# Sparse attention's score products with the queries' high and low parts stacked along the contraction

## Chip, core and metric

The kernel runs on one core of one Trainium2 chip. The metric is the device time of one execution in microseconds (us). TensorE (PE) multiplies, VectorE (DVE), ScalarE (ACT) and GpSimd (POOL) do the elementwise work, and SyncE (SP) issues nearly all DMAs. Every engine runs its own instructions in the order in which they are written and waits on semaphores for the others.

## What is computed

The reference is two transformer blocks in a row on 512 positions of 1024 channels, in float32. The part that the change touches is in the first block: an attention of 8 heads of 64 channels which share one head of keys and values, and in which each query sees only the 128 keys that an indexer has chosen for it.

```python
def dsa_attention(q, k, v, qi, ki, wi):        # q: 8 heads x 64, k and v: one head of 64
    ...
        score = jnp.einsum('bqh,bqhs->bqs', wib.astype(jnp.float32), rel)
        score = jnp.where(causal[None], score, -jnp.inf)
        _, sel = lax.top_k(score, topk)         # topk = 128
        ...
        logits = jnp.einsum('bqhd,bqkd->bqhk', qb, k_sel).astype(jnp.float32) * (HEAD_DIM ** -0.5)
        logits = jnp.where(valid[:, :, None, :], logits, -jnp.inf)
        p = jax.nn.softmax(logits, axis=-1).astype(v.dtype)
        return jnp.einsum('bqhk,bqkd->bqhd', p, v_sel)
```

Beside it stands a second branch of the same block: a gated input `u`, a causal convolution of 31 taps over 4 chunks of 128 channels, a layer norm and a silu. Both branches meet in the product with `w_out`.

## The kernel before

**Numbers in two parts.** A float32 operand is kept as a rounded high part and a low part (the remainder), both of TensorE's fast type. A product of two such operands is three matmuls into one bank: high by high, high by low, low by high. The helper `three` (lines 1556 to 1560) does that, so in the profile the three have the lines L1558, L1559 and L1560 wherever they are used.

**Weights.** `load` (L438) brings a unit of weights into one of two halves of `RAW`; ACT rounds it into `WH` (L550), POOL subtracts it into `WL` (L1113), and PE multiplies (L1436, L1437 with `WH`, then L1442 with `WL`). A load waits until POOL has done the unit two before it (`w_lo`).

**The sparse stage.** It has 32 tiles: 4 groups `c` of 8 tiles `t`. A group is a chunk of 128 query channels, which is two heads; `half = t // 4` chooses the head (64 partitions), `t % 4` the block of 128 queries, and a tile has (t % 4 + 1) * 128 keys. The keys stand twice, in partitions 0 to 63 and 64 to 127 of `KSH` (high) and `KSL` (low). For tile n, PE runs in this order: `scores` of tile n + 3 (three matmuls of 64 rows, and one of 128 rows, L1583, which adds the mask `SEL` through an identity); `convolve_beside`, nine full matmuls of the convolution of chunks 2 and 3 into `ST` (tiles 0 to 10 and 12 to 22); `turn`, the transposes of the softmax of tile n (L1595); and `values`, the products with V for the tiles before. ACT takes the exponentials (L685) and the high part of the turned tile (`PTH`, L697). DVE takes the maximum (`NMX`, L2216), the reciprocal and the scaling (L2221, L2223), the low part (`PTL`, L2228), and per tile for n below 23 one tap of the convolution of chunks 0 and 1 (`CV`, L2128, two instructions).

**POOL beside it.** `diagonals(j)` (L1146) makes eight diagonal matrices of taps, high and low, for PE's convolution; it waits until PE has used the set two before. `queries(c)` (L1189, L1191) splits query chunk c into `AQH[b]` and `AQL[b]`, b = c % 2: chunks 0 and 1 while the weights `memk` are worked on, chunks 2 and 3 between the diagonals. Buffer 0 goes by the names `QSH` and `QSL` in the profile. `scores` waits for `staged` at t = 0.

**SP.** Its list is loads only here: `memk` (8 units), `memv` (8), then `outa` (8 units of `w_out`).

**The later layer ("fox").** In the second block another attention already works with stacked parts: SP copies 64 rows of high and low parts between partitions (`stack`, L511, twelve copies of 128 KB a group; `biases`, L515), and `scores` there is two full-height matmuls (L1585, L1586) and one with an identity (L1587).

Of the kernel before, what the change touches and what calls it, by code (L numbers as in the profile page):

```python
# [16 lines left out]
F32 = mybir.dt.float32  # L17
# [104 lines left out]
def build_program(nc, A, out):  # L122
    ctx = ExitStack()
    with ctx:
        first = (nc.sbuf_base + 127) // 128 * 128

        def at(name, shape, dt, offset):
            return nc.alloc_sbuf_tensor_at(name, shape, dt, offset=first + offset)
# [4 lines left out]
        def sem(name):  # L133
            return ctx.enter_context(nc.semaphore(name))
# [23 lines left out]
        AQH = [QSH[0], at("AQH1", [P, T], F32R, 43008)]  # L158
        AQL = [QSL[0], at("AQL1", [P, T], F32R, 45056)]
# [216 lines left out]
        cvs_in, k_lo = sem("cvs_in"), sem("k_lo")  # L376
# [57 lines left out]
        def _(sp):  # L434
# [16 lines left out]
            for name, w in (("memk", w_k), ("memv", w_v), ("outa", w_out[:, 0:4, :]), ("outb", w_out[:, 4:8, :]),  # L451
# [13 lines left out]
                with sp.Fori(name == "oc", 4) as i:  # L465
                    for s in range(2):
                        load(unit_at(name, i, s), s, w[:, :, bass.ds(i * 2 * P + s * P, P)])
# [642 lines left out]
        def _(pool):  # L1110
# [75 lines left out]
            def queries(c, b, first, last):  # L1186

                free("sparse", c, first)
                pool.tensor_copy(AQH[b][:], DS[:, bass.ds(c + 4, 1), :])  # L1189
                pool.drain()  # L1190
                pool.tensor_tensor(AQL[b][:], DS[:, bass.ds(c + 4, 1), :], AQH[b][:], ALU.subtract).then_inc(staged, 1)  # L1191
# [9 lines left out]
            for j in range(8):  # L1201
                remainder(START["memk"] + j, j % 2)
                if j in (3, 5):
                    queries(j // 4, j // 4, True, False)
# [7 lines left out]
            queries(2, 0, False, False)  # L1212
            for j in range(5, 8):
                diagonals(j)
            queries(3, 1, False, False)
# [209 lines left out]
        def _(pe):  # L1425
# [136 lines left out]
            def scores(kind, c, b, t):  # L1562
# [4 lines left out]
                if kind == "fox":  # L1567
                    if t == 0:
                        pe.wait_ge(stacked[0], 96 * (c + 1))
                        pe.wait_ge(stacked[1], 96 * (c + 1))  # L1570
                        pe.wait_ge(bias_in, 96 if c else 32)
                    if t % TB == 0:
                        pe.wait_ge(staged, STAGED[kind] + 2 * c + half + 1)
                elif t == 0:
                    pe.wait_ge(staged, STAGED[kind] + c + 1)
# [4 lines left out]
                elif kind == "sparse":  # L1580
                    rows = slice(half * 64, half * 64 + 64)
                    three(s[:, 0:nk], AQH[b][rows, q], AQL[b][rows, q], KSH[0][rows, 0:nk], KSL[0][rows, 0:nk], True, False)
# [139 lines left out]
            pe.wait_ge(k_lo, 1)  # L1722
# [1158 lines left out]
```

## Time and profile before

| | us |
|---|---|
| median of 3 runs | 2156.45 (2152.4 to 2157.42) |
| the profiled execution | 2157.53 |
| its span in the trace | 2155.7 |
| PE busy | 1979.7 (92%) |
| DVE busy | 1110.4 (52%) |
| POOL busy | 1047.3 (49%) |
| the sparse stage in the trace, first scores to the last `PTL` | 202 to 319 |

The profile gives starts in us from the start of the span. A matmul's recorded duration includes the time in the array, so what a matmul costs a busy PE is the distance from its start to the start of the next one. PEclk is the clock granted to TensorE as a share of 2.4 GHz; 0.50 is its lower level of 1.2 GHz. "Idle before" is what an engine waited, with the instruction that ended the wait.

### The profile page before, as it was taken

What the parts mean: (1) busy time and instruction counts of PE and PEld (TensorE: products, weight loads), DVE (VectorE), ACT (ScalarE), POOL (GpSimd) and SP (SyncE); (2) the same over time, 40 slices, a digit from 0 to 9 for tenths busy, and PEclk for the clock granted to TensorE, in tenths of its full rate; (3) what the DMA queues carried; (4) which work ended last, traced back from release to release, by engine and by line L of the source; (5) the groups of instructions that cost most, each with busy time, mean ns of one, the idle gap of its engine ahead of it and who ended that gap; (6) DMA issues with size and microseconds to landing.
All of it is one profiled execution on the core that took longest, in us unless ns stands there. A gap on an engine that the chain in (4) does not pass through costs nothing.

```text
span 2155.7 us, 30205 instructions
## 1 busy us (share of the span) xinstructions
PE 1979.7 (92%) x9963; PEld 1603.1 (74%) x9963; DVE 1110.4 (52%) x1820; ACT 733.4 (34%) x1233; POOL 1047.3 (49%) x573
## 2 busy tenths in 40 slices
PE   7888998989999999756899999999997799999997
PEld 5677766768887888545778888887876678888886
DVE  6787873654678696689434223132137844132232
ACT  4323234353322322435442222233235643222223
POOL 5465425526765744680454444446444235444442
PEclk9999999999999999889999999999999999999999
DMA  4233002323332333100233333334345413333332
GB/s 142 71 91 100 1 1 64 98 50 88 97 98 85 94 95 90 56 2 0 69 98 98 89 105 90 98 97 99 97 111 124 112 59 97 98 98 92 103 88 88
DMA packets 343417, 179.52 MB, mean 83 GB/s; under 512 B 27951, under 2 KB 335527, under 8 KB 343335
## 3 DMA queue, kind: packets, MB, share of 16 engines
q1 hardware_dynamic: 342592, 177.81, 29.4%
q8 instruction: 43, 0.70, 0.1%
q10 hardware_dynamic: 742, 0.68, 0.1%
q14 instruction: 40, 0.32, 0.1%
HBM read 162.73 MB, written 2.10 MB: 76 GB/s over the span
## 4 chain that ended last, share of the span: by engine, by line
PE 54%; issue 12%; POOL 9%; DVE 9%; POOLq 6%; DVEq 4%; ACT 4%; DMA 2%; SPq 1%; ACTq 0%
PE ACC L1436 15%; PE ACC L1442 15%; PE ACC L1437 15%; POOL WL L1113 7%; POOLq L1123 2%; DVEq L2222 1%; POOLq L1295 1%; POOLq L1283 1%; DVE PTL L2228 1%; ACT WH L550 1%; DMA RAW<-in_w_v_cross_dram 1%; PE ST L1558 1%; PE ST L1560 1%; PE ST L1559 1%; PE O L1558 1%
## 5 line engine op out<-in xcount | busy, mean ns | idle before, releaser
L1113 POOL TENSOR_TENSOR WL<-RAW,WH 128x1024 fp32r<-128x1024 f32 (+1 forms) x308 | 733.4, 2383 | 792.3 <-ACT WH L550 717.7
L1436 PE MATMUL ACC<-PH,WH 128*128 128x512 f32 x1248 | 495.6, 397 | 11.7 <-DVE PL L1962 3.1
L1437 PE MATMUL ACC<-PL,WH 128*128 128x512 f32 x1248 | 489.5, 392 | 0.0
L550 ACT ACTIVATE WH<-RAW 128x1024 fp32r<-128x1024 f32 (+1 forms) x308 | 317.8, 1034 | 490.1 <-PE ACC L1442 414.4
L1436 PE MATMUL ACC<-QH,WH 128*128 128x512 f32 (+1 forms) x1136 | 431.5, 384 | 23.8 <-ACT WH L550 18.1
L1437 PE MATMUL ACC<-QL,WH 128*128 128x512 f32 (+1 forms) x1136 | 426.8, 380 | 0.0
L1442 PE MATMUL ACC<-PH,WL 128*128 128x512 f32 x1248 | 311.1, 391 | 0.0
L1436 PEld LDWEIGHTS ACC<-PH,WH 128*128 128x128 f32 x1248 | 236.5, 190 | 71.1 <-issue 4.7
L1442 PE MATMUL ACC<-QH,WL 128*128 128x512 f32 (+1 forms) x1136 | 272.3, 380 | 9.6 <-POOL WL L1113 9.4
L1437 PEld LDWEIGHTS ACC<-PL,WH 128*128 128x128 f32 x1248 | 236.6, 190 | 49.3 <-issue 1.0
L1442 PEld LDWEIGHTS ACC<-PH,WL 128*128 128x128 f32 x1248 | 234.0, 188 | 52.6 <-issue 3.3
L1436 PEld LDWEIGHTS ACC<-QH,WH 128*128 128x128 f32 x1136 | 215.4, 190 | 75.6 <-issue 20.4
L1442 PEld LDWEIGHTS ACC<-QH,WL 128*128 128x128 f32 x1136 | 205.4, 189 | 55.2 <-POOL WL L1113 15.7
L1437 PEld LDWEIGHTS ACC<-QL,WH 128*128 128x128 f32 x1136 | 215.5, 190 | 39.0 <-issue 0.2
L2755 DVE TENSOR_TENSOR X<-X,ACC 128x512 f32 x48 | 33.0, 688 | 216.3 <-PE ACC L1442 216.3
L2745 DVE TENSOR_TENSOR H<-ACC,RS 128x512 f32<-128x512 f32 x64 | 44.3, 692 | 147.5 <-PE ACC L1442 147.0
L1122 POOL TENSOR_TENSOR SSQ<-SSQ,SQ 128x512 f32<-128x512 f32 x52 | 75.5, 1453 | 70.6 <-ACT SQ L557 63.8
L757 ACT ACTIVATE QH<-H 128x512 f32 (+1 forms) x54 | 34.2, 633 | 153.4 <-DVE H L2747 128.2
L697 ACT ACTIVATE PTH<-ACC 128x128 fp32r<-128x128 f32 (+2 forms) x112 | 48.1, 429 | 83.3 <-PE O L1560 55.5
L2228 DVE TENSOR_TENSOR PTL<-ACC,PTH 128x128 fp32r<-128x128 f32 (+2 forms) x112 | 53.3, 476 | 31.1 <-ACT PTH L697 30.8
L2128 DVE SCALAR_TENSOR_TENSOR CV<-U,VEC,CV 128x512 f32<-128x512 f32 x60 | 65.5, 1132 | 0.5
L757 ACT ACTIVATE PH<-H 128x512 f32 (+1 forms) x32 | 20.3, 633 | 128.6 <-DVE H L2747 128.6
(416 smaller groups left out, 2436.0 us busy)
## 6 DMA issues: line engine op xcount, KB each, us to landing
RAW<-in_mlp_w_dram SPq DMA_DIRECT2D x128, 512.0 KB, 4.0
RAW<-in_w_gate_dram SPq DMA_DIRECT2D x22, 512.0 KB, 3.7
RAW<-in_w_up_dram SPq DMA_DIRECT2D x22, 512.0 KB, 3.7
RAW<-in_w_in_dram SPq DMA_DIRECT2D x16, 512.0 KB, 3.8
RAW<-in_w_down_dram SPq DMA_DIRECT2D x16, 512.0 KB, 4.0
RAW<-in_ssm_w_glu_dram SPq DMA_DIRECT2D x16, 512.0 KB, 3.8
RAW<-in_w_kvf_dram SPq DMA_DIRECT2D x16, 512.0 KB, 3.9
RAW<-in_w_k_cross_dram SPq DMA_DIRECT2D x8, 512.0 KB, 4.0
```

Of the source, the lines that this page charges most:

```text
L550: act.activation(WH[:, s, 0:kc], RAW[:, s, 0:kc], ACT.Copy).then_inc(w_hi, 1)
L697: act.activation(PTH[:, first:first + kb, qb * P:(qb + 1) * P], TT[t % 2][:, 0:kb * P].rearrange("p (k q) -> p k q", q=P), ACT.Copy).then_ ...
L757: act.activation(hi[:, bass.ds(k, 1), :], to, ACT.Copy).then_inc(hid_hi, 1)
L1113: pool.tensor_tensor(WL[:, s, 0:kc], RAW[:, s, 0:kc], WH[:, s, 0:kc], ALU.subtract).then_inc(w_lo, 1)
L1122: pool.tensor_tensor(SSQ[:], SSQ[:], SQ[:, s, :], ALU.add).then_inc(sq_used, 1)
L1123: pool.drain()
L1436: pe.matmul(ACC[s][:, 0:n], WH[:, s, k, :], xh[:, k, :], start=(k == 0), stop=False)
L1437: pe.matmul(ACC[s][:, 0:n], WH[:, s, k, :], xl[:, k, :], start=False, stop=False)
L1442: mm = pe.matmul(ACC[s][:, 0:n], WL[:, s, k, :], xh[:, k, :], start=False, stop=(k == kc - 1))
L2128: ins = dve.scalar_tensor_tensor(CV[c][:], x, column("conv_b_w", BCH * k + c), CV[c][:], ALU.mult, ALU.add)
L2228: dve.tensor_tensor(PTL[to], TT[t % 2][:, 0:kb * P].rearrange("p (k q) -> p k q", q=P), PTH[to], ALU.subtract).then_inc(pt_lo, 1)
L2745: dve.tensor_tensor(h[:], ACC[s][:], RS[:], ALU.mult).then_inc(unit_out, 1)
```

## The change

The queries' high and low parts are put under one another. For each chunk SP copies 64-row halves of `AQH` and `AQL` into `AQ[b][:, half, :]`, a tile of 128 partitions in which 64 hold the high part of one head and the other 64 its low part (four copies of 128 KB a chunk, semaphore `joined`). Against `KSH`, whose two halves are the same keys, one full-height matmul then gives high by high plus low by high. Against `KLZ[half]`, which holds the keys' low part in the rows of the high queries and zeros in the others, a second gives high by low. `keys_low` on POOL makes `KLZ` once. `queries` no longer waits for exponentials but for the copies to have read its buffer, and SP's list now has the copies of chunks 0 and 1 ahead of the `outa` loads, those of chunks 2 and 3 behind the first two of them, and the other six `outa` loads last.

```diff
+        AQ = [at(f"AQ{b}", [P, 2, T], F32R, x) for b, x in enumerate((176128, 43008))]
+        AQH = [at(f"AQH{b}", [P, T], F32R, 25088 + 4096 * b) for b in range(2)]
+        AQL = [at(f"AQL{b}", [P, T], F32R, 27136 + 4096 * b) for b in range(2)]
+        KLZ = [at("KLZ0", [P, T], F32R, 47104), KSL[0]]
...
+                if name == "outa":
+                    for c in range(4):
+                        if c == 2:
+                            for s in range(2):
+                                load(START[name] + s, s, w[:, :, s * P:(s + 1) * P])
+                        sp.wait_ge(staged, c + 1)
+                        if c >= 2:
+                            sp.wait_ge(e_done, TILES["sparse"] + 8 * (c - 1) + 4)
+                        for u in range(2):
+                            mine, other = own(u), own(1 - u)
+                            for to, src in ((mine, AQH), (other, AQL)):
+                                sp.dma_start(AQ[c % 2][to, u, :].bitcast(F32), src[c % 2][mine, :].bitcast(F32)).then_inc(joined[c % 2], 16)
-                with sp.Fori(name == "oc", 4) as i:
+                with sp.Fori(name in ("outa", "oc"), 4) as i:
...
-            def queries(c, b, first, last):
-
-                free("sparse", c, first)
-                pool.tensor_copy(AQH[b][:], DS[:, bass.ds(c + 4, 1), :])
+            def queries(c):
+
+                if c >= 2:
+                    pool.wait_ge(joined[c % 2], 64)
+                b = c % 2
+                pool.tensor_copy(AQH[b][:], DS[:, c + 4, :])
                 pool.drain()
...
+            def keys_low():
+
+                pool.tensor_copy(KLZ[0][0:64, :], KSL[0][0:64, :].bitcast(F32))
+                pool.drain()
+                pool.memset(KLZ[1][0:64, :].bitcast(F32), 0.0)
+                pool.drain()
+                pool.memset(KLZ[0][64:P, :].bitcast(F32), 0.0)
+                pool.drain().then_inc(k_lo, 1)
...
                 remainder(START["memk"] + j, j % 2)
                 if j in (3, 5):
-                    queries(j // 4, j // 4, True, False)
+                    queries(j // 4)
+                elif j == 1:
+                    keys_low()
...
+                elif t == 0 and kind == "sparse":
+                    pe.wait_ge(joined[c % 2], 64 * (c // 2 + 1))
...
                 elif kind == "sparse":
-                    rows = slice(half * 64, half * 64 + 64)
-                    three(s[:, 0:nk], AQH[b][rows, q], AQL[b][rows, q], KSH[0][rows, 0:nk], KSL[0][rows, 0:nk], True, False)
+                    pe.matmul(s[:, 0:nk], AQ[b][:, half, q], KSH[0][:, 0:nk], start=True, stop=False)
+                    pe.matmul(s[:, 0:nk], AQ[b][:, half, q], KLZ[half][:, 0:nk], start=False, stop=False)
                     mm = pe.matmul(s[:, 0:nk], IDR[:], SEL[:, qb, 0:nk], start=False, stop=True)
```

On PE the block of a tile's scores stands between a turn and the convolution. Here are the turn of tile 0, the scores of tile 4 (128 keys) and the first of the convolution behind them, before:

```order
L1595 MATMUL ACC<-CST,E 128x128
L1558 MATMUL FOUR<-KSH,QSH 128x128
L1559 MATMUL FOUR<-KSL,QSH 128x128
L1560 MATMUL FOUR<-KSH,QSL 128x128
L1583 MATMUL FOUR<-SEL,IDR 128x128
L1558 MATMUL ST<-UH,DGH_120 128x512
```

and in the changed kernel, whose line numbers are higher (`AQ_76` is `AQ[0]`; the second product takes `KSL`, which is `KLZ[1]`, since tile 4 is of the second head):

```order
L1624 MATMUL ACC<-CST,E 128x128
L1610 MATMUL FOUR<-KSH,AQ_76 128x128
L1611 MATMUL FOUR<-KSL,AQ_76 128x128
L1612 MATMUL FOUR<-SEL,IDR 128x128
L1585 MATMUL ST<-UH,DGH_125 128x512
```

One matmul of the four is gone, and the two products left have 128 rows like their neighbours.

On SP the rows behind the last `memv` load are, before, the loop of the `outa` loads:

```order
L438 DMA RAW<-in_w_v_cross_dram 128x8x128
L465 REGISTER_ALU
L465 COMPARE_AND_BRANCH
L465 UNCONDITIONAL_BRANCH
L465 ISA
L438 ISA
L438 DMA RAW<-in_w_out_dram 128x4x128
```

and in the changed kernel:

```order
L478 DMA AQ_76<-AQH_78 64x512
L478 DMA AQ_76<-AQL_80 64x512
L478 DMA AQ_76<-AQH_78 64x512
L478 DMA AQ_76<-AQL_80 64x512
L478 DMA AQ_77<-AQH_79 64x512
L478 DMA AQ_77<-AQL_81 64x512
L478 DMA AQ_77<-AQH_79 64x512
L478 DMA AQ_77<-AQL_81 64x512
L440 DMA RAW<-in_w_out_dram 128x4x128 x2
```

Eight copies now stand between the last `memv` load and the first `outa` load.

## Rows read from the trace of the kernel before

**Rows 1.** Windows of the sparse stage: stretch, its length, busy time by engine, PEclk, DMA.

```profile
202.00:210.00 8.00, 7.95 (x24) 5.59 (x25) 4.07 (x10) 3.10 (x8) 1.92 (x1) 0.66 0.18 53
210.00:247.00 37.00, 37.00 (x177) 27.96 (x175) 31.82 (x56) 10.21 (x31) 15.05 (x9) 0.98 0.00 1
247.00:252.00 5.00, 1.34 (x7) 0.79 (x6) 4.85 (x5) 0.91 (x2) 3.46 (x2) 1.00 0.00 0
252.00:260.00 8.00, 8.00 (x24) 5.55 (x24) 6.48 (x14) 2.42 (x7) 0.00 (x0) 0.57 0.00 0
260.00:302.00 42.00, 42.00 (x207) 31.94 (x207) 36.27 (x73) 13.89 (x41) 10.29 (x6) 1.00 0.00 1
```

**Rows 2.** Timeline of PE: scores of 256, 512 and 128 keys and what follows.

```profile
229.08 0.38 PE L1558 MATMUL FOUR<-KSH,AQH 64*128 64x256 f32 x1
...
229.85 0.40 PE L1558 MATMUL ST<-UH,DGH 128*128 128x512 f32 x1
...
236.64 0.50 PE L1558 MATMUL FOUR<-KSH,AQH 64*128 64x512 f32 x1
...
237.86 0.39 PE L1558 MATMUL ST<-UH,DGH 128*128 128x512 f32 x1
238.10 0.40 PE L1559 MATMUL ST<-UL,DGH 128*128 128x512 f32 x1
...
240.58 0.40 PE L1560 MATMUL O<-PTH,VSL 128*128 128x512 f32 x1
240.91 0.32 PE L1558 MATMUL FOUR<-KSH,AQH 64*128 64x128 f32 x1
...
241.55 0.45 PE L1558 MATMUL ST<-UH,DGH 128*128 128x512 f32 x1
```

**Rows 3.** Timeline of PE in the later layer: full-height scores of 256 keys.

```profile
1634.67 0.28 PE L1585 MATMUL FOUR<-R,L 128*128 128x256 f32 x1
1634.79 0.28 PE L1586 MATMUL FOUR<-R,L 128*128 128x256 f32 x1
```

**Rows 4.** Timelines of DVE, POOL and PE around the wait of tile 11.

```profile
246.31 4.70 DVE L2128 SCALAR_TENSOR_TENSOR CV<-U,VEC,CV 128x512 f32<-128x512 f32 x2
253.12 1.40 DVE L2128 SCALAR_TENSOR_TENSOR CV<-U,VEC,CV 128x512 f32<-128x512 f32 x2
```

```profile
248.10 2.36 POOL L1146 TENSOR_TENSOR DGL<-CST,WCL 128x1024 fp32r<-128x1024 f32 x1
```

```profile
251.87 0.66 PE L1595 MATMUL ACC<-CST,E3sparse 128*128 128x128 f32 x4 [3.66 <-DVE E3sparse L2223]
```

**Rows 5.** Timelines of ACT and PE where the sparse stage begins.

```profile
200.43 1.06 ACT L550 ACTIVATE WH<-RAW 128x1024 fp32r<-128x1024 f32 x1 [1.19 <-DMA RAW<-in_w_out_dram]
201.74 0.38 ACT L674 ACTIVATE VM<-ACC 128x256 f32 x1 [0.25 <-PE ACC L1442]
```

```profile
202.05 0.29 PE L1558 MATMUL FOUR<-KSH,QSH 64*128 64x128 f32 x1 [0.45 <-ACTq L759]
```

**Rows 6.** The later layer's copies: SP's timeline, and a window of them.

```profile
1628.21 0.61 SPq L511 DMA_DIRECT2D R<-KLS  x1
```

```profile
1626.00:1630.00 4.00, 3.86 (x16) 3.27 (x15) 3.55 (x11) 3.12 (x10) 0.00 (x0) 0.50 0.89 204
```

**Rows 7.** Timelines of POOL and ACT in `memk`, and POOL's memset by line.

```profile
151.99 0.61 POOL L1189 CAST QSH<-DS 128x512 fp32r<-128x512 f32 x1
...
153.99 2.38 POOL L1113 TENSOR_TENSOR WL<-RAW,WH 128x1024 fp32r<-128x1024 f32 x1
```

```profile
151.13 1.06 ACT L550 ACTIVATE WH<-RAW 128x1024 fp32r<-128x1024 f32 x1 [1.29 <-DMA RAW<-in_w_k_cross_dram]
```

```profile
L1409 POOL MEMSET VSH<- 128x1024 f32 x1 | 1.0, 952 | 0.2 <-issue 0.2
```

**Rows 8.** Timelines of POOL and PE: chunk 3's queries, and their first use.

```profile
281.74 1.55 POOL L1191 TENSOR_TENSOR AQL<-DS,AQH 128x512 fp32r<-128x512 f32 x1
```

```profile
290.59 0.33 PE L1558 MATMUL FOUR<-KSH,AQH 64*128 64x128 f32 x1
```

More of the change, by code:

```diff
@@ L157, in build_program @@
         VSL = [at("VSL", [P, TB, 2, P], F32R, 190464), at("VSL1", [P, TB, 2, P], F32R, 77824)]
-        AQH = [QSH[0], at("AQH1", [P, T], F32R, 43008)]
-        AQL = [QSL[0], at("AQL1", [P, T], F32R, 45056)]
+        AQ = [at(f"AQ{b}", [P, 2, T], F32R, x) for b, x in enumerate((176128, 43008))]
+        AQH = [at(f"AQH{b}", [P, T], F32R, 25088 + 4096 * b) for b in range(2)]
+        AQL = [at(f"AQL{b}", [P, T], F32R, 27136 + 4096 * b) for b in range(2)]
+        KLZ = [at("KLZ0", [P, T], F32R, 47104), KSL[0]]
         CST = at("CST", [P, NCST], F32, 194560)
@@ L375, in build_program @@
         pv_done = sem("pv_done")
-        cvs_in, k_lo = sem("cvs_in"), sem("k_lo")
+        cvs_in, k_lo, joined = sem("cvs_in"), sem("k_lo"), [sem("joined0"), sem("joined1")]
         staged = sem("staged")
@@ L1184, in free @@
                     pool.wait_ge(e_done, TILES[kind] + SIZE[kind] * (c - 1) + 4)
-            def queries(c, b, first, last):
-                free("sparse", c, first)
-                pool.tensor_copy(AQH[b][:], DS[:, bass.ds(c + 4, 1), :])
-                pool.drain()
-                pool.tensor_tensor(AQL[b][:], DS[:, bass.ds(c + 4, 1), :], AQH[b][:], ALU.subtract).then_inc(staged, 1)
+            def queries(c):
[3 more added lines that the diff above has]
+                pool.tensor_copy(AQH[b][:], DS[:, c + 4, :])
+                pool.drain()
+                pool.tensor_tensor(AQL[b][:], DS[:, c + 4, :], AQH[b][:], ALU.subtract).then_inc(staged, 1)
+            def keys_low():
[5 more added lines that the diff above has]
+                pool.drain().then_inc(k_lo, 1)
             def inputs_low(j):
@@ L1211, in _ @@
                 diagonals(j)
-            queries(2, 0, False, False)
+            queries(2)
             for j in range(5, 8):
                 diagonals(j)
-            queries(3, 1, False, False)
+            queries(3)
             for c in range(BCH):
@@ L1721, in _ @@
             pe.wait_ge(sel_ready, TB)
-            pe.wait_ge(k_lo, 1)
+            pe.wait_ge(k_lo, 2)
             pe.wait_ge(v_lo, 2)
```

## The prediction

> **What bounds the kernel now.** The change lives in one stage of the span, so I read the windows of that stage first and then the timelines of single engines in it. In [rows 1] PE is busy for 37.00 of 37 us from 210 to 247 and for 42.00 of 42 from 260 to 302: there PE alone sets the pace. From 247 to 252 it is busy for 1.34 us only. The reader should look at DVE beside it: 31.82 of 37, 4.85 of 5, 6.48 of 8 and 36.27 of 42 us. DVE is the second bound, close behind, and PE's hole at 247 is its doing: PE waits 3.66 us for the scaled exponentials of tile 11 [rows 4]. DVE is late there because two taps of the convolution took 4.70 us where the same two take 1.40 seven microseconds later; POOL made diagonals just then, and the taps' end comes right after the end of POOL's instruction (248.10 + 2.36 = 250.46) [rows 4]. Behind that hole the granted clock is 0.57 from 252 to 260, and it is 0.66 from 202 to 210 [rows 1].
>
> **What PE loses.** The cost of a block of scores is the distance from its first matmul to the first of the convolution [rows 2]: 241.55 - 240.91 = 0.64 us for 128 keys, 229.85 - 229.08 = 0.77 for 256, 237.86 - 236.64 = 1.22 for 512, and about 1.00 for 384, taken between its neighbours. The matmul ahead of the block is stretched too: 240.91 - 240.58 = 0.33 instead of 0.24 (238.10 - 237.86, same width). That 0.09 I give to every block. A full-height block is three matmuls like those of the later layer: 0.12 each for 256 keys (1634.79 - 1634.67) [rows 3] and, since that looks like a floor, 0.12 for 128; 0.24 for 512, and 0.18 for 384 between them. So the blocks become 0.36, 0.36, 0.54 and 0.72. The saving of four tiles is 0.28 + 0.41 + 0.46 + 0.50 + 4 x 0.09 = 2.0 us, and eight such fours make **16 us of PE's time** at the full clock.
>
> Most of this is not the matmul that goes. The third matmul itself is 0.12 + 0.12 + 0.18 + 0.24 = 0.66 us of each 2.0, 5.3 of the 16. The rest is what PE loses where it goes from 128 rows to 64 and back: about 0.1 us ahead of the block, 0.1 in its first matmul, and 0.1 to 0.2 at the mask matmul. These are my reading of the distances; no row before shows a full-height block inside the sparse stage.
>
> The Trainium skill, page "TensorEngine Tiling (Array Packing)", section Tiling Modes, says that going to another tiling mode drains TensorE. By that rule the border costs are real and vanish with the 64-row matmuls; without it the change would be worth only the 5.3 us of the third matmuls.
>
> **What of it reaches the end.** *The first four blocks* run back to back from 202.05 and nothing else is due: DVE is busy for 4.07 of 8 us [rows 1]. All of their 2.0 us counts, and since the clock falls among them I take **2.7** (bounds 2.0 to 4.0, all at full or all at half clock). *From 210 to 302* PE saves 24 blocks, 12 us. DVE has 12.6 us free in these 92 (5.2 + 0.15 + 1.5 + 5.7, [rows 1]), part of it the short gaps between its own instructions. So PE and DVE would be level, and level engines which hand each tile back and forth do not both run full. It is worse while POOL makes diagonals, which happens six times in the stage: a pair blocks DVE for some 2 to 3.3 us (4.70 - 1.40, [rows 4]), and PE uses up a set of eight taps in 2.67 tiles. In those tiles DVE is the bound as soon as PE is any faster. The room is in the tiles without diagonals. I take **2.5** (bounds 0 and 10: nothing, or DVE's free time less its own gaps), nearer to nothing because the only hole of PE that the trace has, [rows 4], is DVE's and stays. *After 302* four blocks are left, among waits of PE for DVE and ACT: **0.3**. Together 5.5 us.
>
> The Trainium skill, page "SBUF — State Buffer", on the SBUF ports, says that DVE and GpSimd share a pair of ports under an exclusive lock and the loser is blocked for the whole instruction. The trace agrees (4.70 us where 1.40 is usual [rows 4]). By that rule alone a faster PE buys nothing while POOL works; without it I would put the middle term near its upper bound.
>
> **What it adds.** *Copies ahead of the load.* SP issues a copy in 0.61 us, and while copies run, the queues move 204 GB/s at a share of 0.89 [rows 6]. Eight copies behind the last `memv` load take 8 x 0.64 = 5.1 us of SP, from about 193 to 198, where the first `outa` load went out at 197.6: 0.5 us late. Their 1.05 MB take 5.1 us of the queues, behind or among the 0.5 MB of that `memv` load, so the queues are free at about 200 to 201.5, and the `outa` unit may land 0.5 to 2.2 us later than at 200.43. Behind it in ACT's order stand the rounding (1.06 us) and the copy of `VM`, which has 0.25 us to spare, and PE's first scores wait for the semaphore that follows it [rows 5]. That puts the whole stage back by 0.3 to 2; I take **1.3**. The new wait on `joined` stands at the same place; chunk 0's four copies should have landed by about 199, so it is not last.
>
> *`keys_low`.* One copy of half the rows (0.61 for 128 rows of 512 [rows 7]; I count it whole), two memsets of 512 columns (half of 0.95 each [rows 7]) and three drains of some 0.15: 2.0 us on POOL behind unit 1 of `memk`. Unit 2's remainder comes 2.0 later, hence the load of unit 4 too. Unit 4 was rounded at 151.13 + 1.06 = 152.2, and POOL took it at 153.99 only [rows 7], since `queries(0)` stood ahead: 1.8 us of cover. What is left is 0.2; I take **0.3** (bounds 0 and 2.0, the cover gone).
>
> *Chunk 3.* Its low part is ready at 281.74 + 1.55 = 283.3 and PE wants it at 290.59 [rows 8]: 7.3 us. SP's wait, four issues and the landing take 0.1 + 4 x 0.64 + about 2 = 4.6, and PE gains up to 2 between. It is covered by 0.7 us or so; PE would stop in front of it with the convolution and the turn queued behind, and I price that at 0 (bounds 0 to 1). Chunk 2 has over 10 us. The six `outa` loads now go out at about 285 instead of 204; the first of them is needed after 320, and it costs nothing. `queries` of chunks 2 and 3 waits for copies long landed.
>
> Sum: -5.5 + 1.3 + 0.3 = **-3.9 us**. Against the profiled execution's 2157.5 that is 2153.6; its time is 1.1 above the median of the runs, so from the median it is 2152.5. I say 2153. A measurement of this kernel can tell about 0.3%, 6.5 us, from no change, so this counts as no change.
>
> **Rivals.** (A) *PE's gain goes through.* DVE was held up by PE, not only beside it, and the diagonals fall elsewhere: the middle term is 9, the clock does not fall at the start, which saves 1 more, and the time is 2156.5 - 2.7 - 1 - 9 - 0.3 + 1.6 = 2145. For it: DVE has 12.6 us free [rows 1]. Against: the lock. Chance 0.25. (B) *Only the third matmul counts.* The borders' 0.1 us are not due to the height; PE saves 5.3 in all, some 2 reach the end, less 1.6 of costs: 2156. The distances of [rows 2] speak against it. Chance 0.12. (C) *The clock falls more often: slower than before.* PE gets some 12 us of new waits for DVE. Behind the wait of 3.66 us [rows 4] eight microseconds ran at 0.57 [rows 1]; each such stretch costs PE about 3.4 us, of which DVE's slowness covers little. One more makes 2156, two 2159.5, three 2163; it is slower than before from the second on. Against: in the 79 us in which PE runs full the clock is 0.98 to 1.00, and the waits that I expect are spread and most of them shorter than that one. Chance 0.15 for one or two more, 0.06 for three. (D) *The `outa` load is 4 us late*, with the copies in front of all of it, 2155.5: chance 0.07. The forecast itself has 0.35.
>
> **How the numbers follow.** Faster by over 0.3% (below 2150) is A with the lower edge of the forecast, 0.28. Slower by over 0.3% (above 2163) is C with three stretches and what I have not seen, 0.08. The rest, 0.64, is within 0.3%. The range reaches from the near side of A to C with two stretches and some spread: 2146.5 to 2161.
>
> **What would show it.** In the profile after: blocks of scores of 0.36 and 0.72 us for 128 and 512 keys; the first scores at 203 to 204 instead of 202.05; DVE busy for nearly all of 212 to 300 with PE's waits named after the scaled exponentials or `PTL`; the turns of tile 3 some 1.5 us earlier than before and those of tile 25 some 4. The prediction is wrong if PE stays busy to the full (then B), if DVE's busy time shrinks (A), or if PEclk shows further stretches near 0.5 (C).

## The result, and the profile after

| | before | after |
|---|---|---|
| median, us | 2156.9 (5 runs, 2152.4 to 2157.5) | 2144.9 (5 runs, 2142.3 to 2145.3) |
| the profiled execution, its span | 2157.5, 2155.7 | 2142.3, 2140.5 |
| PE busy | 1979.7 | 1962.5 |
| DVE busy | 1110.4 | 1108.7 |
| POOL busy | 1047.3 | 1048.8 |

The ratio of the times is 0.9945 (95% interval 0.9931 to 0.9958): the change is 12.0 us faster, three times what was forecast (3.9) and below the range. Timed again beside the last experiments its ratio was 0.9958 (0.9943 to 0.9973). The first interval lies wholly below 0.997, so the change is faster by more than the 0.3% that can be told from none; the second alone, which reaches 0.9973, would leave that just open. The two share 0.9943 to 0.9958, 9 to 12 us.

Windows of the changed kernel, the stretches of [rows 1] (stretch, length, busy time and instructions of PE, PE's loads, DVE, ACT, POOL, then PEclk, DMA share, GB/s):

```profile
202.00:204.00 2.00, 1.32 (x10) 1.09 (x9) 0.00 (x0) 0.76 (x1) 0.23 (x1) 1.00 0.24 61
204.00:210.00 6.00, 6.00 (x32) 5.16 (x33) 4.12 (x11) 3.73 (x11) 2.40 (x1) 1.00 0.10 31
210.00:247.00 37.00, 30.89 (x158) 24.36 (x156) 35.54 (x56) 10.57 (x31) 18.49 (x10) 1.00 0.06 15
247.00:252.00 5.00, 2.92 (x8) 2.08 (x9) 4.70 (x11) 1.93 (x5) 0.00 (x0) 0.50 0.00 0
252.00:260.00 8.00, 8.00 (x38) 6.63 (x37) 6.84 (x16) 2.42 (x8) 0.00 (x0) 0.89 0.01 2
260.00:302.00 42.00, 38.37 (x200) 30.29 (x199) 37.49 (x76) 14.93 (x43) 10.38 (x6) 1.00 0.08 19
```

Three things differ from [rows 1]. The clock from 204 to 210 is 1.00, where 202 to 210 had 0.66. PE, which had been busy for 37.00 of 37 us, is busy for 30.89, and DVE has risen from 31.82 to 35.54. The hole near 247 and the lower clock behind it are still there, a little earlier.

The blocks of scores are as short as forecast. PE's timeline of the first four blocks (128, 256, 384, 512 keys), of the convolution behind them and of tile 0's turn:

```profile
203.95 0.30 PE L1610 MATMUL FOUR<-KSH,AQ 128*128 128x128 f32 x1 [0.45 <-ACTq L773]
...
204.31 0.33 PE L1610 MATMUL FOUR<-KSH,AQ 128*128 128x256 f32 x1
...
204.72 0.34 PE L1610 MATMUL FOUR<-KSH,AQ 128*128 128x384 f32 x1
...
205.25 0.40 PE L1610 MATMUL FOUR<-KSH,AQ 128*128 128x512 f32 x1
...
205.94 0.40 PE L1585 MATMUL ST<-UH,DGH 128*128 128x512 f32 x1
...
208.04 0.27 PE L1624 MATMUL ACC<-CST,E 128*128 128x128 f32 x1
```

0.36, 0.41, 0.53 and 0.69 us, 1.99 together; the forecast was 0.36, 0.36, 0.54 and 0.72, 1.98. What PE waited for from the turn of tile 0 to that of tile 22 (times in us, count, longest), where the kernel before had one wait (last line, from its own turns of tiles 0 and 22):

```profile
PE ACC L1624 <- DVE E2sparse L2252: 3.6, 3, 2.3
PE ACC L1624 <- DVE E3sparse L2252: 3.5, 2, 2.0
PE ACC L1624 <- DVE E L2252: 1.2, 1, 1.2
PE O L1585 <- DVE PTL L2257: 0.8, 3, 0.3
```

```profile
PE ACC L1595 <- DVE E3sparse L2223: 3.7, 1, 3.7
```

All of it is DVE's, before and after.

**A table of distances.** Times in a trace shift by some 2 us from execution to execution before the stage begins, so I compare distances between starts inside of it. *Start*: from the rounding of `memv`'s unit 6 to the first scores. *First*: from there to the turn of tile 0. Then turn of tile 0 to 11, 11 to 22, turn of tile 22 to the last tile's `PTL`, and from that to the next rounding of weights and on to the seventh after it. All in us, one trace each; the kernels of the experiments stand here too, and the last column is the ratio of their time to that of the kernel before, timed beside them.

| kernel | start | first | 0 to 11 | 11 to 22 | 22 to end | behind | on | ratio |
|---|---|---|---|---|---|---|---|---|
| before | 8.1 | 8.7 | 41.1 | 43.8 | 22.5 | 4.8 | 27.9 | |
| before_again | 9.1 | 8.8 | 41.0 | 43.8 | 22.6 | 4.7 | 27.8 | |
| after | 9.8 | 4.1 | 41.0 | 38.8 | 22.6 | 3.4 | 26.7 | 0.9945 |
| after_again | 9.8 | 4.1 | 40.9 | 38.8 | 22.6 | 3.4 | 26.7 | |
| after_five | 10.0 | 4.1 | 40.7 | 38.7 | 23.0 | 4.1 | 26.4 | 0.9958 |
| third_full | 9.7 | 4.7 | 39.2 | 39.3 | 22.4 | 3.4 | 26.5 | 0.9962 |
| first_four_64 | 9.8 | 7.6 | 39.3 | 38.8 | 22.6 | 3.4 | 26.7 | 0.9980 |
| rest_64 | 9.5 | 4.1 | 40.8 | 43.8 | 22.9 | 4.2 | 26.5 | 0.9991 |
| all_64 | 11.8 | 8.9 | 40.9 | 43.8 | 22.8 | 4.3 | 27.9 | 1.0006 |
| last_four_64 | 10.2 | 4.1 | 40.9 | 38.7 | 23.5 | 3.4 | 26.3 | |
| before_two_64 | 8.1 | 6.9 | 40.8 | 43.8 | 22.9 | 4.2 | 26.5 | 0.9997 |
| before_act_scales | 9.1 | 8.9 | 37.6 | 41.7 | 25.9 | 5.3 | 27.3 | 0.9984 |
| act_scales | 10.4 | 4.1 | 35.9 | 37.1 | 26.8 | 4.4 | 26.7 | 0.9958 |
| act_scales_23 | 10.6 | 4.1 | 35.8 | 37.8 | 22.9 | 4.9 | 26.7 | 0.9929 |
| chunk1_late | 9.8 | 4.1 | 40.5 | 38.6 | 22.6 | 3.4 | 27.8 | 0.9960 |
| copies_behind | 9.2 | 4.1 | 39.3 | 38.8 | 22.6 | 3.4 | 26.7 | 0.9953 |
| both | 9.2 | 4.1 | 35.8 | 36.9 | 23.4 | 4.3 | 26.4 | 0.9930 |
| no_diagonals | 10.4 | 4.1 | 32.0 | 36.0 | 22.4 | 3.4 | 27.9 | 0.9920 |

From before to after (first two rows against the next two) the sum is: start +1.2, first -4.7, 0 to 11 nothing, 11 to 22 -5.0, 22 to end nothing, behind -1.3, on -1.1. That is -10.9 of the 9 to 12.

### The profile page after: what moved, and what is told of

It reads as the page before. It is cut to its first block, busy times and chain, and to the rows that moved or that the text cites. A ratio compares the mean times of both kernels' runs of the same rounds, so it can differ in the third digit from the quotient of the medians.

```text
span 2140.5 us, 30157 instructions
## 1 busy us (share of the span) xinstructions
PE 1962.5 (92%) x9931; PEld 1595.0 (75%) x9931; DVE 1108.7 (52%) x1820; ACT 732.9 (34%) x1233; POOL 1048.8 (49%) x576
## 4 chain that ended last, share of the span: by engine, by line
PE 51%; issue 13%; DVE 10%; POOL 9%; POOLq 6%; DVEq 4%; ACT 4%; DMA 2%; SPq 1%; ACTq 0%
PE ACC L1463 16%; PE ACC L1469 15%; PE ACC L1464 15%; POOL WL L1127 7%; POOLq L1137 2%; DVE CV L2157 2%; DVE PTL L2257 1%; DVEq L2251 1%; POOLq L1310 1%; POOLq L1322 1%; ACT WH L564 1%; DVEq L2161 1%; DVE NMX L2245 1%; PE ST L1903 1%; POOL GC L1321 1%
## 5 line engine op out<-in xcount | busy, mean ns | idle before, releaser
L1463 PE MATMUL ACC<-PH,WH 128*128 128x512 f32 x1248 | 494.9, 397 | 10.2 <-DVE PL L1991 2.4
```

Of the source, the lines that this page charges most:

```text
L1463: pe.matmul(ACC[s][:, 0:n], WH[:, s, k, :], xh[:, k, :], start=(k == 0), stop=False)
```

## Experiments

### Second traces

The two kernels unchanged, and the changed one timed again.

> The kernel before once more, for a second trace. Theory 1 (the stretches at the lower clock belong to the kernel): the granted clock falls again at 204, 252, 316, 344, 382 and 416 us, 30.6 us of stretches that cost 15.3 us of PE time between 200 and 430. Theory 2 (they fall by chance from execution to execution): the first one at 204 or the three behind 340 are elsewhere or missing, and the landmarks of the sparse stage move by 2 to 5 us against the first trace.

> The changed kernel once more, for a second trace. Theory 1: the clock is at its full level from 202 to 245, falls once behind PE's holes at 246 and once at 336, and nowhere else up to 420. Theory 2: a stretch at the lower clock stands among the first four blocks of scores in this trace, the turn of tile 0 comes at 210 to 211 instead of 208.0, and the time is still 2142 to 2146, so that the clock is not where the gain is.

> The changed kernel unchanged, timed again beside the others: 10 to 12 us below the kernel before by the sum of the distances (1.2 later at the start, 4.7 and 5.1 to 6 less in the stage, 2.4 less behind it), first scores 9.8 us behind the rounding of unit 6, 4.1 us to the turn of tile 0, 101 to 102.5 from there to the low part of the last tile.

Theory 1 holds for the stage. Windows of before_again, with its first scores at 205.1:

```profile
204.00:206.00 2.00, 1.55 (x11) 1.23 (x10) 0.12 (x1) 1.22 (x2) 1.85 (x1) 1.00 0.04 13
206.00:214.00 8.00, 8.00 (x22) 5.22 (x21) 3.95 (x10) 2.14 (x7) 0.00 (x0) 0.59 0.11 33
```

The fall of the clock among the first blocks is there again, and none in after_again and after_five. Those near 252 (246 in the changed kernel), 320 and 346 came again too; the ones at 382 and 416 did not, and after_again had one at 218 that the first trace had not. So the distances in the stage repeat to 0.1 us in the second traces (to 0.4 in after_five, the third of the changed kernel), and those behind it move by 1 to 3 us with where the clock falls. Two timings of the same change that read 0.9945 and 0.9958 are within such a spread; that this is their reason is not shown.

### One half of the edit undone

first_four_64 gives tiles 0 to 3 their 64-row products back, as the diff shows; rest_64 all others (`c or t >= 4`, with the 64 rows of the tile's own half); all_64 every tile, so that only the additions are left.

```diff
                 if c >= 2:
                     pool.wait_ge(joined[c % 2], 64)
+                    pool.wait_ge(e_done, TILES["sparse"] + 8)
...
-                    pe.matmul(s[:, 0:nk], AQ[b][:, half, q], KSH[0][:, 0:nk], start=True, stop=False)
-                    pe.matmul(s[:, 0:nk], AQ[b][:, half, q], KLZ[half][:, 0:nk], start=False, stop=False)
+                    if c == 0 and t < 4:
+                        rows = slice(0, 64)
+                        three(s[:, 0:nk], AQH[b][rows, q], AQL[b][rows, q], KSH[0][rows, 0:nk], KLZ[0][rows, 0:nk], True, False)
+                    else:
...
```

PE then reads `AQH` and `AQL` itself, so POOL's `queries` has to wait for it again before it writes them; in rest_64 and all_64 that wait is the kernel before's own, `free("sparse", c, False)`.

> The changed kernel, but the scores of the first four tiles are three matmuls of 64 rows each, as before; everything else, waits and copies too, is that of the changed kernel. If the height of these four blocks only costs what their lengths say, the time rises by 2.0 us to about 2147, and the clock stays at its full level there. If these blocks are also what lets the clock fall from 204 on (0.55 of full speed for 6 us before), the stretch at the lower clock is back, the turn of tile 0 moves from 208.0 to about 212.5, and the time rises by 4.5 us, to 2149.5.

> The other half of the edit undone: the first four tiles' scores are stacked, those of tiles 4 to 31 are three matmuls of 64 rows. If the gain of the first blocks and of the middle are separate, the distance from the first scores to the turn of tile 0 is 4.1 us as in the changed kernel, and from that turn to the low part of the last tile it is 107.4 us as before, not 102.3; the time is 2149 to 2150. If the middle's gain came from the earlier start (DVE's work running ahead), this distance is again 102 to 103 us, and the time is near 2145.

> The changed kernel with its copies, waits and keys_low, but all 32 tiles' scores are three matmuls of 64 rows. What is left of the change is what it adds. By the traces so far the first scores come 1.2 us later (9.9 us behind the rounding of the weights' unit 6 instead of 8.6) and nothing else moves: distances of 7.6 to 8.8 and 107.4 us in the stage as before, a stretch at the lower clock in the first blocks, and 1 to 1.5 us more than the kernel before. The verdicts of the two halves (2.3 and 4.3 us faster alone, 12 together) would rather say 5 us more.

The two halves are separate by the distances. In rest_64 the first part stays at 4.1 us and tiles 11 to 22 take 43.8 as before; in first_four_64 it is the other way round, 7.6 and 38.8. Of the 3.5 us between 7.6 and 4.1, 1.7 are clock, by the window in which it fell (5 us at 0.66):

```profile
209.00:214.00 5.00, 5.00 (x18) 3.76 (x17) 3.00 (x7) 0.89 (x4) 0.00 (x0) 0.66 0.00 0
```

and 1.8 are the length of the blocks; the prediction's 2.0 was about right. all_64 shows the price of the additions: its median is 1.6 us above that of the kernel before, as forecast, and far from 5; its ratio, 1.0006 (0.9995 to 1.0017), does not tell it from nothing. The ratios of the halves, 4.3 us for first_four_64 and 1.9 for rest_64, and the additions, which each of them pays, make 7 to 8 us together, somewhat less than the change's own 9 to 12. Its start of 11.8 is later than expected (9.9); the clock fell for a while between 200 and 204 as well. And rest_64 bounds what 64 rows do to the clock: from tile 4 on it has such blocks one at a time between nine matmuls of the convolution, and from the turn of tile 0 to that of tile 11 its clock is 1.00.

### A third product of full height

```diff
                     pe.matmul(s[:, 0:nk], AQ[b][:, half, q], KLZ[half][:, 0:nk], start=False, stop=False)
+                    pe.matmul(s[:, 0:nk], AQ[b][:, half, q], KLZ[1 - half][:, 0:nk], start=False, stop=False)
```

> The changed kernel with a third full-height product per tile (queries times the keys' other half of KLZ, which adds low by low): the same count of matmuls as before, but all of 128 rows. It adds 0.12, 0.12, 0.18 and 0.24 us of PE per four tiles, 5.3 us in all. If PE's time sets the pace of the middle, the time rises by all of it, to 2150. If DVE sets the pace, only the first four blocks (0.7 us) and a few of the last count, and it rises by 1 to 2 us, to about 2146.5.

The first part is 0.6 us longer, 4.7. From the turn of tile 0 to that of tile 22 it is 78.5 us, not more than the changed kernel's 79.8, although PE has 3.6 us more to do there; only in the second half are there 0.5 us more. The first half, 39.2 for 41.0, flatters it: first_four_64 and copies_behind have 39.3 there with the changed kernel's own matmuls, and DVE is busy for 37.6 us in third_full and in copies_behind where it is for 39.2 in the changed kernel. It depends on how the taps meet POOL's diagonals. Against these two, the stretch is 0.5 us longer. So most of the 3.6 us is hidden: PE no longer sets the pace over that stretch as a whole. The ratio, 0.9962 (0.9949 to 0.9976), can't be told from that of the changed kernel. It also parts the 1.8 us of the blocks: 0.6 is the third matmul, 1.2 the 64 rows, which the distances of [rows 2] put at the borders between 64 and 128 rows. The rule of the Trainium skill that the prediction weighed (page "TensorEngine Tiling (Array Packing)", Tiling Modes: a change of tiling mode drains TensorE) agrees with that. Rival B, that only the third matmul counts, is out.

### Which property of the first blocks lets the clock fall

In the kernel before, the first four tiles without their third product:

```diff
+                    if c == 0 and t < 4:
+                        pe.matmul(s[:, 0:nk], AQH[b][rows, q], KSH[0][rows, 0:nk], start=True, stop=False)
+                        pe.matmul(s[:, 0:nk], AQH[b][rows, q], KSL[0][rows, 0:nk], start=False, stop=False)
+                    else:
...
```

> The kernel before, but the scores of the first four tiles leave out the third product (low queries by high keys), so that they are two matmuls of 64 rows and one of 128. If the length of these blocks or their number of matmuls lets the clock fall at 204 to 206, the clock stays at its full level there and the distance from the first scores to the turn of tile 0 is 8.7 - 0.7 - 3.1 = 4.9 to 5.3 us. If the 64-row matmuls do it, the stretch at the lower clock is still there and the distance is 7.6 to 8.1 us.

The result lies between the two: 6.9 us. The clock fell, at 206, and was back before 210, where in the kernel before it fell at 204.6 and was back before 212:

```profile
203.00:206.00 3.00, 3.00 (x12) 1.75 (x12) 2.02 (x6) 2.44 (x6) 1.55 (x1) 1.00 0.06 17
206.00:210.00 4.00, 4.00 (x12) 2.93 (x11) 2.11 (x5) 0.42 (x3) 0.00 (x0) 0.57 0.19 56
```

The third product of 64 rows isn't needed for the fall. third_full has as many matmuls as the kernel before, of as many columns, but of 128 rows, and its clock stays up (the half microsecond of idle PE in this window is the wait ahead of the first scores at 204.47):

```profile
204.00:210.00 6.00, 5.53 (x32) 4.90 (x33) 3.31 (x9) 4.47 (x10) 2.39 (x1) 1.00 0.13 39
```

Over all traces here: the six in which the first four blocks have 64-row matmuls all show the fall between first scores and the turn of tile 0 (1.7 to 3.4 us lost), and the twelve with full-height blocks show none. In first_four_64 against the changed kernel nothing else on PE differs. So the height of these blocks decides it, in this kernel. Whether it is the fewer rows themselves, or the time lost between heights, isn't told apart.

The same for the last tiles:

```diff
+                    if c == 3 and t >= 4:
+                        rows = slice(half * 64, half * 64 + 64)
+                        three(s[:, 0:nk], AQH[b][rows, q], AQL[b][rows, q], KSH[0][rows, 0:nk], KLZ[half][rows, 0:nk], True, False)
+                    else:
...
```

> The changed kernel, but tiles 28 to 31 have 64-row products. If full-height products there are why the clock no longer falls around 316 us, a stretch at the lower clock of 3.4 us appears at 304 to 314, and from the low part of the last tile to the next rounding of weights it is 4.2 to 4.8 us instead of 3.4. If it comes from the stage ending earlier, the distance stays at 3.4 and no stretch appears.

A stretch of the lower clock did appear, at 305 to 309, but ahead of the last `PTL` (311.98), and the distance behind the stage stayed 3.4; after_five has full-height tiles, such a stretch at 306 to 310, and 4.1 behind. So the height of these tiles does not decide it.

What the 1.3 us behind the stage are can be read across the traces: they are the clock. In the eight traces whose granted clock is 1.00 from the last `PTL` to the next rounding, that distance is 3.41 to 3.43; in the ten others it is 4.1 to 5.3, and 3.3 to 3.6 once what the lower clock cost is taken off. The column *on* goes the same way: 27.8 or 27.9 in the five traces with a clock of 0.89 there, two of which are variants of the changed kernel (chunk1_late, no_diagonals), and 26.3 to 26.7 in all others but one (27.3). before_two_64, a variant of the kernel before, has 26.5. Where the clock falls behind the stage thus differs among executions and variants on either side, and the 2.4 us are not shown to belong to the edit. The windows behind the last `PTL`, before and after:

```profile
318.00:323.00 5.00, 4.47 (x18) 3.58 (x17) 0.69 (x1) 1.17 (x3) 1.27 (x1) 0.73 0.01 3
```

```profile
310.00:316.00 6.00, 4.59 (x24) 3.70 (x23) 1.39 (x2) 1.97 (x4) 2.71 (x3) 1.00 0.01 3
```

### Work taken off DVE

The scaling of the exponentials goes to ACT (DVE keeps the reciprocal), in the changed kernel and in the kernel before.

```diff
+            def scaled(n, t):
+                nk, j = keys("sparse", t), t % SLOTS["sparse"]
+                act.wait_ge(rec_ready, 16 + n + 1)
+                act.activation(E4["sparse"][j][:, 0:nk], E4["sparse"][j][:, 0:nk], ACT.Copy,
+                               scale=REC[:, j, :]).then_inc(e_scaled, 1)
...
                         n = 8 * c + t
+                        scaled(n, t)
```

> The changed kernel, with the scaling of the exponentials moved from DVE to ACT in the sparse stage (DVE still makes the reciprocal). It takes 32 instructions, 18.4 us in the trace of the changed kernel between 206 and 311, off DVE. If DVE sets the pace of the changed kernel from the first scores to the end of the stage, PE's waits (some 12 us between 210 and 302) mostly go, the stage gets 7 to 10 us shorter and the time is about 2137. If PE or the hand-over between the engines sets the pace, the longer way over ACT costs what it saves, and the time stays at 2144 to 2146.

> The kernel before with the same move of the scaling to ACT. If PE set its pace in the middle (busy 79 of 79 us outside of the hole at 247), only the hole of 3.7 us and perhaps the stretch at the lower clock behind it can go: 3 to 6 us faster. If DVE bounded the kernel before as well, it gains as much as the changed kernel does, 7 to 10 us.

In the changed kernel tiles 0 to 11 went from 41.0 to 35.9 us and 11 to 22 from 38.8 to 37.1: DVE had set the pace of the first half. In the kernel before, 0 to 11 lost 3.4 us, its one hole, and 11 to 22 went from 43.8 to 41.7: the lower clock behind the hole is gone (1.00 from tile 11 to tile 22). So DVE bounded the kernel before at tile 11 too, and PE bounded the rest. But act_scales ended at 2141.8, not 2137, with the same ratio as the changed kernel in after_five (0.9958): the part after tile 22 grew from 22.6 to 26.8. There DVE has no taps left, and I took the way over ACT to be only longer. Leaving tiles 23 to 31 to DVE was the next run.

> The changed kernel with the scaling on ACT for tiles 0 to 22 only; DVE scales tiles 23 to 31 itself, since it has no taps any more there. With all 32 tiles on ACT the distance from the turn of tile 22 to the low part of the last tile was 26.8 us against 22.6, with 5.1 us lost to the lower clock between 298 and 310. If the longer way over ACT in these last tiles made the new holes of PE, the distance is back at 22.6 and the time is 4 us below that run, about 2138. If the holes come from PE having caught up with DVE and ACT anyway, it stays at 26 to 27 and the time at 2141 to 2142.

Windows from the turn of tile 22 to the end, all on ACT and then with DVE from tile 23:

```profile
281.00:309.00 28.00, 20.07 (x89) 14.36 (x89) 13.16 (x34) 16.45 (x42) 3.60 (x4) 0.83 0.00 1
```

```profile
283.00:307.00 24.00, 19.01 (x89) 13.22 (x88) 17.93 (x43) 12.24 (x33) 3.27 (x4) 0.90 0.01 1
```

22.9 us instead of 26.8. The clock is higher in this window too, but it is not the reason: `both`, below, has these tiles on DVE as well, a clock as low as act_scales (0.82 and 0.85 from the turn of tile 22 to the last `PTL`), and needs 23.4. The median is 2137.4 and the ratio 0.9929 (0.9916 to 0.9943), where it was 0.9958 (0.9943 to 0.9973) with all tiles on ACT.

### The lock

POOL leaves out its diagonals of the stage, and PE multiplies with old ones.

```diff
                 if j >= 2:
                     pool.wait_ge(diag_used, j - 1)
+                if j >= 2:
+                    pool.sem_inc(diag_ready, 1)
+                    return
```

> The changed kernel, but POOL leaves out the six pairs of diagonal matrices of the sparse stage (it only signals; TensorE multiplies with old ones, so the convolution of chunks 2 and 3 is left wrong). If POOL's work beside DVE is what stretches the taps (0.99 us each in the mean where 0.70 is usual), the 46 taps fall to about 0.70, DVE has 13 to 15 us less to do, and the distance from the turn of tile 0 to that of tile 22 falls from 79.8 to 68 to 72 us, where PE's own work ends it. If POOL's share is small, it stays above 77.

From the turn of tile 0 to that of tile 22, the taps of the changed kernel and of this one (count, busy us, mean ns):

```profile
L2157 DVE SCALAR_TENSOR_TENSOR CV<-U,VEC,CV 128x512 f32<-128x512 f32 x45 | 43.1, 997 | 0.0
```

```profile
L2160 DVE SCALAR_TENSOR_TENSOR CV<-U,VEC,CV 128x512 f32<-128x512 f32 x45 | 32.0, 753 | 0.0
```

and the windows of tiles 0 to 11 and 11 to 22 without the diagonals:

```profile
209.90:241.90 32.00, 31.48 (x168) 26.39 (x166) 28.59 (x65) 11.37 (x34) 1.90 (x2) 1.00 0.08 17
241.90:277.90 36.00, 35.26 (x183) 29.41 (x184) 32.50 (x70) 12.89 (x37) 2.49 (x2) 1.00 0.09 23
```

POOL's work costs DVE 11 us of its taps, and the stretch is 11.8 us shorter (68.0 for 79.8): PE is busy for all but 1.3 us, the hole and the lower clock behind it are gone. The median is 2137.2 (0.9920, 0.9904 to 0.9936). Beside POOL, the taps' ends follow POOL's. In the changed kernel eight pairs of taps took longer than 1.4 us between the turns of tiles 0 and 22, and each ended 0.53 to 0.55 or 1.21 us after the end of one of POOL's instructions (here 224.25 + 3.77 = 228.02 and 225.34 + 2.15 = 227.49):

```profile
224.25 3.77 DVE L2157 SCALAR_TENSOR_TENSOR CV<-U,VEC,CV 128x512 f32<-128x512 f32 x2
```

```profile
225.34 2.15 POOL L1160 TENSOR_TENSOR DGL<-CST,WCL 128x896 fp32r<-128x896 f32 x1
```

The exclusive lock that the Trainium skill's page "SBUF — State Buffer" describes (section "SBUF: two separate sides") agrees with these ends, and the 11 us are its size here.

### The place of the copies

Chunk 1's copies behind the first two `outa` loads (chunk1_late):

```diff
-                        if c == 2:
+                        if c == 1:
                             for s in range(2):
                                 load(START[name] + s, s, w[:, :, s * P:(s + 1) * P])
```

One load, chunk 0's copies, the second load, chunk 1's copies (copies_behind; `both` has act_scales_23's move besides):

```diff
-                        if c == 2:
-                            for s in range(2):
-                                load(START[name] + s, s, w[:, :, s * P:(s + 1) * P])
+                        if c < 2:
+                            load(START[name] + c, c, w[:, :, c * P:(c + 1) * P])
```

> The changed kernel, but SP issues the four copies of chunk 1 behind the first two loads of w_out, so that four copies instead of eight stand in front of them. If the issues of SP and the bytes of the copies make the stage start late (first scores 1.4 to 1.9 us later than before), half of it or more comes back: first scores about 1 to 1.5 us earlier, 2143.5 us. If four copies are enough for the whole delay, or DVE's taps have to be done first anyway, nothing moves, 2145.

> The changed kernel, with SP's list: first load of w_out, four copies of chunk 0, second load of w_out, four copies of chunk 1. With the copies ahead of the load, the last unit of the value weights was rounded 4.4 to 4.6 us after the one before it, against 1.6 to 2.8 in the kernel before, whether four or eight copies stood there. If the copies slow that unit's own transfer, this distance falls to 1.6 to 2.8 again, the first scores come 1 to 1.5 us earlier measured from the rounding of unit 6 (8.2 to 8.8 instead of 9.8), and the time falls by 1 us. The new risk is that the first scores then wait for chunk 0's copies, which land at about 202.5: then the start stays at 9.5 to 10.

> Both of these changes in one kernel: if each does what it should, the stage from the rounding of unit 6 to the low part of the last tile takes 9 + 4.1 + 95.6 us, and the time is about 2137. If DVE's lock with POOL or PE's clock takes it back, it stays at 2141.

chunk1_late left the start at 9.8: it isn't the `outa` load that is late. ACT's timeline in the changed kernel, the roundings of `memv`'s units 6 and 7 and of the first `outa` unit:

```profile
194.14 1.06 ACT L564 ACTIVATE WH<-RAW 128x1024 fp32r<-128x1024 f32 x1 [2.55 <-DMA RAW<-in_w_v_cross_dram]
...
198.70 1.06 ACT L564 ACTIVATE WH<-RAW 128x1024 fp32r<-128x1024 f32 x1 [3.23 <-DMA RAW<-in_w_v_cross_dram]
...
203.24 1.06 ACT L564 ACTIVATE WH<-RAW 128x1024 fp32r<-128x1024 f32 x1 [3.20 <-DMA RAW<-in_w_out_dram]
```

The load of unit 7 was issued ahead of every copy:

```profile
193.44 0.37 SPq L440 DMA_DIRECT2D RAW<-in_w_v_cross_dram  x1
194.03 0.54 SPq L478 DMA_DIRECT2D AQ<-AQH  x1
```

Still it is rounded 4.6 us after unit 6; in the kernel before it was 2.7 and 1.5. From the end of its issue on SP to its rounding it is 4.8 to 5.7 us in the twelve traces with copies right behind it, and 3.1 to 3.8 in the six without. With the copies behind the first `outa` load the distance between the units is 2.9 (3.2 in `both`), and what stands in front of the first scores is now the other risk named there:

```profile
191.33 1.06 ACT L563 ACTIVATE WH<-RAW 128x1024 fp32r<-128x1024 f32 x1 [2.45 <-DMA RAW<-in_w_v_cross_dram]
...
194.26 1.06 ACT L563 ACTIVATE WH<-RAW 128x1024 fp32r<-128x1024 f32 x1 [1.60 <-DMA RAW<-in_w_v_cross_dram]
```

```profile
200.51 0.30 PE L1609 MATMUL FOUR<-KSH,AQ 128*128 128x128 f32 x1 [1.28 <-DMA AQ<-AQL]
```

So only 0.6 us of the start came back (9.2 for 9.8), less than a timing can tell. Together with the scaling on ACT (`both`) the median is 2137.1, the ratio 0.9930 (0.9917 to 0.9944): no better than act_scales_23. These two are the best versions that ran, 15 us below the kernel before.

## Why the prediction was wrong

**The costs came out right, one of them by luck.** `keys_low` at 0.3: `memv`'s unit 6 is rounded at 194.1, 193.6 and 192.0 in the three traces of the changed kernel, and at 193.9 and 195.9 in the two of the kernel before; nothing of it can be seen. The start at +1.3: +1.2. The reason given was wrong, though, and the size is luck. It was to be the `outa` load; it is the last `memv` load, which the copies behind it slow. Chunk 3 cost nothing, as said. The additions alone measure +1.6 in the medians, the sum of the prediction, with an interval that includes nothing.

**The lengths of the blocks were right,** 1.99 for 1.98, and so was the reading that most of the saving is not the matmul that goes (0.6 of 1.8).

**The first step that failed is the clock's part of the first term.** The term was 2.7 (bounds 2.0 to 4.0), and it measured 4.7. The bounds priced the blocks' own lengths at either clock, and took for granted that the clock falls as it did. But the lower clock lay mainly on the nine convolution matmuls behind the blocks, and it fell because of the blocks: with full height it doesn't fall. From the first scores to the turn of tile 0 the kernel before had

```profile
202.05:210.76 8.71, 8.71 (x26) 6.01 (x26) 4.07 (x10) 3.05 (x8) 1.87 (x1) 0.65 0.16 47
```

8.71 us at 0.65: 3.0 us of clock, on an engine that alone sets the pace there, and 1.6 are left for the lengths. The term held 0.7 of the clock's 3.0. [rows 1], 8 us at 0.66, had shown most of it. The forecast did not price the case that the cause goes with the edit; rival A had the clock staying up, at 1 us.

**The second is the middle, put at 2.5; it measured 5.0.** The bounds of 0 and 10 held, but the choice "nearer to nothing" treated 92 us as one. Taken apart at the hole the answer is plain. Windows from turn 0 to 11 and from 11 to 22, before:

```profile
210.80:251.90 41.10, 37.44 (x180) 28.19 (x178) 36.56 (x60) 11.11 (x32) 18.51 (x10) 0.99 0.00 1
251.90:295.70 43.80, 43.80 (x195) 33.01 (x196) 37.32 (x71) 12.50 (x37) 10.29 (x6) 0.92 0.00 1
```

and after:

```profile
208.00:249.00 41.00, 32.89 (x169) 26.07 (x167) 39.24 (x65) 11.13 (x33) 18.49 (x10) 0.97 0.06 14
249.00:287.80 38.80, 37.76 (x184) 30.82 (x185) 36.29 (x70) 12.68 (x36) 10.38 (x6) 0.94 0.09 21
```

In the first half POOL is busy for 18.5 us. DVE decides where tile 11 comes, before and after, and PE's 4.6 us less of work turned into 4.5 us more of waits (41.1 - 37.4 = 3.7 before, 8.1 after): the prediction's argument from the lock, and it was right, there. (Of the changed kernel's variants with the same taps and matmuls, copies_behind and first_four_64 had 39.3 in this half, so the nothing is not exact.) In the second half POOL is busy for 10.3 us, PE for 43.80 of 43.8, and DVE has 6.5 us free. There the argument does not hold: eleven blocks save 5.5 us of PE by the forecast's prices, and 5.0 arrive. They are made up of some 4.9 us less of PE's work at the full clock, 1.2 less of clock (43.8 us at 0.92, then 38.8 at 0.94: after, the lower clock began at 246.5, partly in DVE's half) and 1.0 more of waits. "Level engines do not both run full" failed as a step; PE is at 37.76 of 38.8 with DVE at 36.29. The 0.3 for the end of the stage was nothing.

**The third is what was not in the sum at all,** 2.4 us behind the stage. The 1.3 us right behind it are the clock, and the 1.1 after them go with it. It is not shown that they belong to the change.

**The signs.** DVE was busy for 35.54 of 37 us and 37.49 of 42, PE's waits bear the names that were forecast, and the first scores came at 203.95. But the turn of tile 3 came 2.9 us earlier (220.7, then 217.8) and not 1.5, which by itself says that the first term was too small, and that of tile 25 came 7.8 us earlier (301.3, then 293.6) and not 4.

**The rivals.** A named the time (2145) by sizes that made up for each other: its first part was 3.7 (4.7 measured), its middle 9 (5.0), and it had nothing behind the stage (2.4). The sign that was named for it, a shrinking busy time of DVE, did not appear. Its mechanism was half right: the clock did not fall, and PE's gain went through after tile 11, not before. C, more falls of the clock, had the sign wrong: PE did get some 4.5 us more of waits, but lost less to the clock. B is out by third_full. D is out by the start, 1.2 us (its time would be 2155.2 by the sum, not 2155.5).

## What to carry to other kernels

Where a bottleneck alternates, cut the stretch at its holes and ask in each part who ends it; a saving on an engine can be worth next to nothing in one and nearly all of itself in the next. A stretch at the lower clock on the engine that sets the pace is a term of its own, with two cases: the cause stays, or it goes with the edit. And when work is moved off a loaded engine, move it only for as long as that engine is loaded: the same move cost some 4 us in the tiles after it.

## What the runs showed of the hardware

- With blocks of 64-row matmuls at the start of the stage the granted clock fell from 2.4 to 1.2 GHz among them or right behind them in six traces of six, with PE recorded busy throughout; with 128-row matmuls in these blocks it fell in none of twelve, and one of the twelve (third_full) has as many matmuls of as many columns. PE's busy time does not tell the two apart. 64-row blocks one at a time between nine matmuls of 128 rows did not do it (clock 1.00 for 40.8 us in rest_64).
- A load that was issued before eight or four copies within the chip landed later for them: 4.8 to 5.7 us from its issue to the rounding that waits for it in twelve traces, instead of 3.1 to 3.8 in six. An earlier place in the queue did not protect it.
- POOL's diagonals, 24.5 us of its busy time between the turns of tiles 0 and 22 (28.9 with them, 4.4 without), cost DVE's 45 taps there 11 us (997 for 753 ns each). All eight stretched pairs ended 0.53 to 0.55 or 1.21 us behind the end of one of POOL's instructions.
